# Turning q and k rows by a DMA transpose instead of TensorE, in the last stack of a one-core kernel

## The chip, the cores and the metric

The kernel runs on one NeuronCore of a Trainium2 chip, as one launch. The metric is the time on the device in microseconds. The kernel before takes 2354.93 us, the median of three runs (2354.59 to 2355.26).

## What is computed

256 tokens of width 2048, all in f32, go through two blocks. The first is a mixer (a gMLP branch and a neighbourhood attention) with a convolved feed-forward. The second has two layers, a gated delta net and a chunked band attention. The change is in that last layer. Cut to what matters:

```python
def chunk_band_attention(h, w_in, q_norm_w, k_norm_w, rel_bias, w_out):
    proj = h @ w_in                                  # 2048 -> 4 * 2048: q, k, v, z
    q = rms_norm_2(proj[..., :B_INNER].reshape(bsz, t, B_HEADS, B_HEAD_DIM), q_norm_w)
    k = rms_norm_2(proj[..., B_INNER:2 * B_INNER].reshape(...), k_norm_w)
    ...
    s = einsum('bchd,bmhd->bhcm', q_n, k_n) * scale + bias    # per chunk of 64 rows, a band of 9 chunks
    p = softmax(s)
    o = einsum('bhcm,bmhd->bchd', p, v_n) * silu(z)
    return o @ w_out
```

There are 16 heads of 128 columns, and the norm is over the 128 columns of a head. The scores contract over these columns, so q and k must lie with the columns of a head on the partitions; the projection leaves them with the tokens on the partitions.

## The kernel before

**Weights.** Every product of rows with a weight matrix is made in split precision. Weights come in halves: here 2 x 128 rows by 512 columns, 512 KB, loaded by SyncE into one of four slots of `raw` (`RAW = 4`). ScalarE copies a half to `w_hi` in fp32r (`act_half`, L494), VectorE subtracts to get `w_lo` (`dve_half`, L504), each into one of four slots (`SPLIT = 4`), and TensorE makes 12 matmuls of a half (`pe_half`, L559 to L561): three products for each of two row blocks of 128 tokens. A tile is a 512-column slice of the result over all 2048 rows of weight, 8 halves, 96 matmuls, in two PSUM banks `G[t % 2]`. SyncE loads a half when `lo_done` says that its slot is free; ScalarE splits half m when TensorE has finished half m - 4.

**Order.** Each engine has one queue, written out by hand. `run(half, n, side, group)` issues n halves and after each one takes one step of each generator given; `yield` ends a step. The generators of the engines are counted so that the steps fit together. ScalarE and VectorE are two halves ahead of TensorE in this order (`LOOK = 2`): their call c of a tile prepares its half c + 2.

**The last stack** is `stack(T_B, rows_side, band, ...)`. For each of four groups of four heads it makes four tiles: q, k, v and z, then three more groups in a loop. After the q tile has ended, `read_rows` scales it out of PSUM to `tok` (ScalarE one row block, VectorE the other), and the next tile, k, runs with `rows_side(gi, 0)` beside it; the v tile runs with `rows_side(gi, 1)`, which treats k. Below, a tile is named by the rows that are treated beside it. `band(gi)` (scores, softmax, values) starts in the z tile and is stretched over the next two tiles, so that its last steps stand beside the q rows of the next group; its first eight steps are empty.

`rows_side` before, call by call: (1) ScalarE sums the squares of `tok`; (2) VectorE makes the mean, ScalarE the root; (3) VectorE takes the reciprocal and scales `tok`, `b_normed`; (4) TensorE turns `tok` by 8 transposes into `AX[0]` and `AX[1]` (`turn_rows`, L1939), `b_turned`; (5) ScalarE copies one bank (L1157), VectorE the other (L1873), to `bqT` or `bkT`, with the norm weight of q or k as scale, `b_out0` and `b_out1`. The scores wait for these at the ninth step of `band`. ScalarE's twentieth step of `band` writes `zT_hi` (L1183), for which VectorE's `zT_lo` waits (L1917); both stand in call 4 of the tile in which the q rows are treated.

Of the kernel before, what the change touches and what calls it, by code (L numbers as in the profile page):

```python
# [13 lines left out]

F32 = mybir.dt.float32
F32R = mybir.dt.float32r
ACT = mybir.ActivationFunctionType
ALU = mybir.AluOpType
AX_X = mybir.AxisListType.X
# [2 lines left out]
P = 128  # L22
T = 256
TB = T // P
D = 2048
# [97 lines left out]
def program(nc, ins, out, parts=4):  # L123
    last_tile = {1: T_UP1, 2: T_A, 3: T_B, 4: N_TILES}[parts]
    last_half = TILE_END[last_tile - 1]
    with ExitStack() as ctx:
# [14 lines left out]
        class Region:  # L141
# [4 lines left out]

            def put(self, name, shape, dt=F32):
                t = nc.alloc_sbuf_tensor_at(name, shape, dt, offset=self.at)
                self.at += nbytes(shape)
                assert self.at <= self.end, (name, self.at, self.end)  # L150
                return t

# [145 lines left out]
        def parts_of(ap, l, h):  # L298
# [18 lines left out]
                     (ins[n][0] for n in ("w_in", "w_branch", "w_out", "w_up", "w_down", "a_w_in_2", "a_w_out_2",  # L317
                                          "b_w_in_2", "b_w_out_2"))))
        bsq = r.put("bsquares", [P, TB, 512])


        SKEW, BAND = 7 * P, 2 * P + C
        na_skew = nc.dram_tensor("na_bias_copies", (NAH, GRID, SKEW), F32, kind="Internal").ap()
        root_rows = nc.dram_tensor("root_rows", (P, TB), F32, kind="Internal").ap()
        gc_rows = nc.dram_tensor("gc_rows", (TB, H, P), F32, kind="Internal").ap()
        band_skew = nc.dram_tensor("band_bias_copies", (H, C, BAND), F32, kind="Internal").ap()

        block = ctx.enter_context(nc.Block())
# [186 lines left out]
        def pe_half(pe, pl):  # L515

            m = pl.m
            if m >= last_half:
                return
            h = HALVES[m]  # L520
            t, w = h["tile"], h["width"]
            if h["start"] and t == IN_AUX[0]:
                pe.wait_ge(S("d_v_rows"), 8)
            elif h["start"] and t == IN_AUX[1]:
                pe.wait_ge(S("b_out0"), 8)
                pe.wait_ge(S("b_out1"), 8)
            elif h["start"] and t >= 2:
                for tb in range(TB):
                    pe.wait_ge(S(f"read_out{tb}"), pl.tiles(t - 1))
            pe.wait_ge(S("lo_done"), pl.halves(m + 1))  # L530
            hi, lo = {"h": (hT_hi, hT_lo), "y": (yT_hi, yT_lo), "m": (mT_hi, mT_lo), "z": (zT_hi, zT_lo)}[h["act"]]
            _, wh, wl = slots(m)
            if is_up(t):
                def low():
                    for k in range(h["n"]):
                        for i in range(w // P):
                            nc.tensor.matmul(up_banks(t)[i][:, 0:T], wl[:, k, i * P:(i + 1) * P], hT[:, h["kt"] + k, 0, :],  # L537
                                             start=False, stop=False)

                if not h["start"]:  # L540
                    low()
                for k in range(h["n"]):
                    for i in range(w // P):
                        mm = nc.tensor.matmul(up_banks(t)[i][:, :], wh[:, k, i * P:(i + 1) * P],  # L544
                                              hT[:, h["kt"] + k, :, :].rearrange("p a t -> p (a t)"),
                                              start=h["start"] and k == 0, stop=h["stop"] and k == h["n"] - 1)
                if h["start"]:
                    for k in range(h["n"]):
                        for i in range(w // P):
                            mm = nc.tensor.matmul(up_banks(t)[i][:, 0:T], wl[:, k, i * P:(i + 1) * P], hT[:, h["kt"] + k, 0, :],  # L550
                                                  start=False, stop=False)
            order = [(k, tb) for k in range(h["n"]) for tb in range(TB)]
            if t == N_TILES - 1 and h["stop"]:
                order.sort(key=lambda at: at[1])
            for k, tb in () if is_up(t) else order:
                xh = hi[:, h["kt"] + k, tb * P:(tb + 1) * P]
                xl = lo[:, h["kt"] + k, tb * P:(tb + 1) * P]
                dst = (AX[tb] if t in IN_AUX else G[t % 2][tb])[:, 0:w]
                nc.tensor.matmul(dst, xh, wl[:, k, :], start=h["start"] and k == 0, stop=False)  # L559
                nc.tensor.matmul(dst, xh, wh[:, k, :], start=False, stop=False)  # L560
                mm = nc.tensor.matmul(dst, xl, wh[:, k, :], start=False, stop=h["stop"] and k == h["n"] - 1)  # L561
                if t == N_TILES - 1 and h["stop"] and (k, tb) == (h["n"] - 1, 0):
                    mm.then_inc(S("first_rows"), 1)
            mm.then_inc(S("half_done"), 1)
            pl.m += 1
# [111 lines left out]
        def _(act):  # L677
# [236 lines left out]
            if parts >= 2:  # L914
                act.wait_ge(S("read_out1"), T_UP1 - 3)
                act.wait_ge(S("consts_landed"), 16 * 10)
                copy_bias(band_skew, ins["b_rel_bias_2"], 2 * REL + 1, "band_copied", 0, H)
                act.dma_start(nf[:, :], ins["norm_final"].partition_broadcast(P)).then_inc(S("nf_landed"), 16)
                feed_forward(T_UP1, 0, UP1, DOWN1, 0)
                act.dma_start(alog[:, :], ins["a_a_log_2"][0].partition_broadcast(P)).then_inc(S("ab_landed"), 16)  # L920
                act.dma_start(dtb[:, :], ins["a_dt_bias_2"][0].partition_broadcast(P)).then_inc(S("ab_landed"), 16)
                act.dma_start(wab[:, :, :], W["a_in"][:, 4 * D:].rearrange("(k p) n -> p k n", p=P)).then_inc(S("wab_landed"), 16)
                feed_forward(T_UP2, UP1, UP2, DOWN2, 1)

            def sums_of_squares(src, dst, junk, event=None, after=None, blocks=range(TB)):
# [171 lines left out]
            def decays():  # L1097
# [4 lines left out]
                A(abT[:, :], AX[3][:, 0:T], ACT.Copy).then_inc(S("ab_out"), 1)  # L1102
                yield
                yield
                act.wait_ge(S("ab_landed"), 32)
                A(alog[:, :], alog[:, :], ACT.Exp)
                act.wait_ge(S("ab_sum"), 1)
                A(beta[:, :, :], gx[:, :, :], ACT.Abs)
# [34 lines left out]
            def rows_side(gi, part):  # L1143
# [7 lines left out]
                A(bss[:, :, :], bss[:, :, :], ACT.Sqrt).then_inc(S("b_root"), 1)  # L1151
                yield
                yield
                yield
                act.wait_ge(S("b_turned"), n + 1)
                for e in range(2):
                    i = A((bqT, bkT)[part][:, e, :], AX[0][:, e * T:(e + 1) * T], ACT.Copy,  # L1157
                          scale=head_gains[:, 1 + part:2 + part])
                i.then_inc(S("b_out0"), 1)
                yield  # L1160

            def band(gi):
                for _ in range(8):
                    yield
                for pr in range(2):
                    n = gi * 2 + pr
# [25 lines left out]
        def _(dve):  # L1192
# [87 lines left out]
            def mixing():  # L1280
# [10 lines left out]
                dve.wait_ge(S("gains_landed"), 16 * 4)  # L1291
                V.tensor_tensor(gains[:, 2, :], gains[:, 2, :], gains[:, 4, :], ALU.mult)
                dve.wait_ge(S("consts_landed"), 16 * 10)
                dve.wait_ge(S("ln_sd"), 1)
                V.reciprocal(lnr[:, :], lnr[:, :])
                dve.drain()
# [441 lines left out]
                e.then_inc(S("z_lo"), 1)  # L1738
                yield

            def read_rows(t, part, bufs, norm):
                if part < 3:
                    tile_done(dve, pl, t)
                    V.tensor_scalar(bufs[part][:, 1, :], G[t % 2][1][:, :], rstd[:, norm, 1:2], None,
                                    ALU.mult).then_inc(S("read_out1"), 1)

            def stack(t0, side, group, bufs, norm, first, second, out_turned):
                for part in range(3):
                    run(half, 8, second if part else none, side(0, part - 1) if part else first)
                    if part == 0:  # L1750
                        finish(first)
                    read_rows(t0 + part, part, bufs, norm)
                finish(second)
                with dve.Fori(0, 3) as i:
                    pl.enter(i, t0 + 3, 4)
# [2 lines left out]
                    for part in range(3):  # L1758
                        run(half, 8, g, side(i + 1, part - 1) if part else side(i, 2))
                        if part == 2:  # L1760
                            finish(g)
                        read_rows(t0 + 4 + part, part, bufs, norm)
                    pl.leave(3)
                g, s = group(3), side(3, 2)
                run(half, 6, g)
# [46 lines left out]
            def decays():  # L1812
# [1 line left out]
                    yield  # L1814
                ab = AX[2][:, 0:TB * 2 * H].rearrange("p (t c) -> p t c", t=TB)
                dve.wait_ge(S("ab_turned"), 1)
                dve.wait_ge(S("ab_landed"), 32)
                for tb in range(TB):
                    e = V.scalar_tensor_tensor(out=gx[:, tb, :], in0=ab[:, tb, 0:H], scalar=rstd[:, 3, tb:tb + 1], in1=dtb[:, :],
                                               op0=ALU.mult, op1=ALU.add)  # L1820
# [37 lines left out]
            def rows_side(gi, part):  # L1858
                n = gi * 2 + part
                if part == 2:  # L1860
# [8 lines left out]
                scaled(tok, tok, bss[:, :, :]).then_inc(S("b_normed"), 1)  # L1869
                yield  # L1870
                yield
                dve.wait_ge(S("b_turned"), n + 1)
                V.tensor_scalar((bqT, bkT)[part][:, 2:4, :], AX[1][:, :].rearrange("p (a t) -> p a t", a=2),  # L1873
                                head_gains[:, 1 + part:2 + part], None, ALU.mult).then_inc(S("b_out1"), 1)
                yield

            def band(gi):
# [49 lines left out]
        def _(pe):  # L1927
# [372 lines left out]

            def decays():

                pe.wait_ge(S("wab_landed"), 16)
                for kt in range(0, KD, 4):
                    for h_part in (hT_hi, hT_lo):
                        for j in range(4):
# [39 lines left out]
                finish(turn_x(2, 3, T_A - 1))  # L2346

            def rows_side(gi, part):
                if part == 2:
                    return  # L2350
                n = gi * 2 + part
                yield
                yield
                yield
                pe.wait_ge(S("b_normed"), n + 1)
                if not isinstance(gi, int) or gi or part:
                    pe.wait_ge(S("b_out0"), n)
                    pe.wait_ge(S("b_out1"), n)
                turn_rows(tok, (0, 1), "b_turned")
                yield  # L2360
                yield

            def band(gi):
                for _ in range(8):
                    yield
                for pr in range(2):
                    n = gi * 2 + pr
                    if pr == 0:
                        pe.wait_ge(S("b_out0"), gi * 2 + 2)
                        pe.wait_ge(S("b_out1"), gi * 2 + 2)  # L2370
                        pe.wait_ge(S("read_out0"), gi * 4 + (T_B + 3))
                        pe.wait_ge(S("read_out1"), gi * 4 + (T_B + 3))
                        pe.wait_ge(S("z_lo"), gi + 4)
# [79 lines left out]
```

## Time and profile before

| | before |
|---|---|
| median of 3 runs | 2354.93 us |
| profiled execution: span from first to last instruction | 2353.4 us |
| own time of the profiled execution | not recorded apart; all runs are within 2354.59 to 2355.26 us |
| TensorE busy | 2343.1 us |
| VectorE busy | 1516.3 us |
| ScalarE busy | 1223.8 us |
| weight and other loads, main DMA queue | 57.6% of 16 engines |

Times in the profile are microseconds from the start of the span. PE is TensorE's matmuls, PEld its weight loads, DVE is VectorE, ACT is ScalarE, ACTq and SPq are the instructions of a queue that issue DMAs. In a timeline a row gives start, duration, engine, line, operation, output and inputs, count, and in brackets the idle time before it with what ended it. Matmuls are pipelined: their durations overlap, and their starts give the pace.

### The profile page before, as it was taken

The page shows a single profiled execution, that of the slowest core. Times are in us where ns is not written, and L with a number is a line of the kernel's source. Part 1 is how long each engine was busy: PE and PEld are TensorE (multiplying, and loading weights), DVE is VectorE, ACT ScalarE, POOL GpSimd, SP SyncE. Part 2 cuts the span into 40 slices and gives each one's busy share as a digit, 9 for nine tenths or more (in the row PEclk, how much of TensorE's full clock was granted, in tenths as well). Part 3 has the DMA queues.
Part 4 walks back from the last instruction along what each step waited for, and adds up shares of the span by engine and source line. Part 5 has one row for each costly group of instructions (what it writes and reads, how often), then busy time and mean ns, then how long its engine had stood idle before and what let it go on. Part 6 is the DMA issues. An engine that isn't in the chain of part 4 may idle for free.

```text
span 2353.4 us, 35087 instructions
## 1 busy us (share of the span) xinstructions
PE 2343.1 (100%) x12183; PEld 1963.4 (83%) x12183; DVE 1516.3 (64%) x2146; ACT 1223.8 (52%) x1931; POOL 68.7 (3%) x92
## 2 busy tenths in 40 slices
PE   9999999999999999999999999999999999999999
PEld 7887788888888888888888878888887888888887
DVE  5657655556577775477776668787876755555554
ACT  5445544444465554355554475756465455555543
POOL 0011200000200000000000000000000000000000
PEclk9999999999999999999999999999999999999999
DMA  8665555565656656566655655555554575656555
GB/s 272 219 207 178 171 190 190 180 200 185 222 179 196 193 183 199 182 196 188 194 184 189 192 154 169 153 169 151 161 149 148 180 223 163 193 155 187 169 169 171
DMA packets 289497, 432.66 MB, mean 184 GB/s; under 512 B 32976, under 2 KB 129136, under 8 KB 289264
## 3 DMA queue, kind: packets, MB, share of 16 engines
q1 hardware_dynamic: 282976, 422.69, 57.6%
q10 hardware_dynamic: 6416, 8.56, 1.1%
q8 instruction: 66, 1.08, 0.2%
q14 instruction: 39, 0.32, 0.0%
HBM read 429.07 MB, written 7.10 MB: 185 GB/s over the span
## 4 chain that ended last, share of the span: by engine, by line
PE 95%; DVE 2%; ACT 1%; DVEq 1%; issue 0%; DMA 0%; ACTq 0%
PE gemm L559 22%; PE gemm L561 22%; PE gemm L560 22%; PE gemm L544 7%; PE aux L544 7%; PE gemm L537 3%; PE aux L537 3%; PE aux L1939 2%; DVE w_lo L504 1%; PE aux L561 1%; PE aux L560 1%; PE aux L559 1%; ACT w_hi L494 1%; PE aux L2180 0%; PE aux L2399 0%; PE aux L2380 0%
## 5 line engine op out<-in xcount | busy, mean ns | idle before, releaser
L504 DVE TENSOR_TENSOR w_lo<-raw,w_hi 128x1024 fp32r<-128x1024 f32 (+1 forms) x800 | 958.1, 1206 | 572.3 <-ACT w_hi L494 567.4
L494 ACT ACTIVATE w_hi<-raw 128x1024 fp32r<-128x1024 f32 (+1 forms) x800 | 815.6, 1042 | 506.0 <-PE gemm L561 402.7
L559 PE MATMUL gemm<-w_lo,hT 128*128 128x512 f32 x1600 | 637.0, 398 | 0.7 <-DVE hT L1224 0.6
L561 PE MATMUL gemm<-w_hi,hT 128*128 128x512 f32 x1600 | 624.0, 390 | 0.0
L560 PE MATMUL gemm<-w_hi,hT 128*128 128x512 f32 x1600 | 623.3, 390 | 0.0
L559 PEld LDWEIGHTS gemm<-w_lo,hT 128*128 128x128 f32 x1600 | 300.6, 188 | 64.8 <-issue 4.1
L561 PEld LDWEIGHTS gemm<-w_hi,hT 128*128 128x128 f32 x1600 | 300.3, 188 | 63.8
L560 PEld LDWEIGHTS gemm<-w_hi,hT 128*128 128x128 f32 x1600 | 300.8, 188 | 58.8 <-issue 0.2
L544 PE MATMUL gemm<-hT,w_hi 128*128 128x512 f32 x704 | 218.5, 393 | 0.1
L544 PE MATMUL aux<-hT,w_hi 128*128 128x512 f32 x672 | 208.0, 390 | 0.0
L559 PE MATMUL gemm<-w_lo,yT_hi 128*128 128x512 f32 x472 | 184.3, 390 | 0.5 <-DVE yT_lo L1467 0.5
L561 PE MATMUL gemm<-w_hi,yT_lo 128*128 128x512 f32 x472 | 183.7, 389 | 0.0
L560 PE MATMUL gemm<-w_hi,yT_hi 128*128 128x512 f32 x472 | 183.6, 389 | 0.0
L544 PEld LDWEIGHTS aux<-hT,w_hi 128*128 128x128 f32 x672 | 126.2, 188 | 28.5
L544 PEld LDWEIGHTS gemm<-hT,w_hi 128*128 128x128 f32 x704 | 122.3, 190 | 17.0 <-issue 0.5
L537 PE MATMUL gemm<-hT,w_lo 128*128 128x256 f32 x616 | 122.1, 282 | 0.0
L537 PE MATMUL aux<-hT,w_lo 128*128 128x256 f32 x588 | 118.5, 283 | 0.0
L537 PEld LDWEIGHTS gemm<-hT,w_lo 128*128 128x128 f32 x616 | 103.9, 190 | 10.2
L559 PEld LDWEIGHTS gemm<-w_lo,yT_hi 128*128 128x128 f32 x472 | 88.6, 188 | 19.8 <-DVE yT_lo L1467 0.9
L561 PEld LDWEIGHTS gemm<-w_hi,yT_lo 128*128 128x128 f32 x472 | 88.6, 188 | 18.6
L560 PEld LDWEIGHTS gemm<-w_hi,yT_hi 128*128 128x128 f32 x472 | 88.6, 188 | 18.1
L537 PEld LDWEIGHTS aux<-hT,w_lo 128*128 128x128 f32 x588 | 91.3, 191 | 0.0
(341 smaller groups left out, 2283.4 us busy)
## 6 DMA issues: line engine op xcount, KB each, us to landing
raw<-in_w_up SPq DMA_DIRECT2D x336, 256.0 KB, 2.9
raw<-in_w_in SPq DMA_DIRECT2D x144, 512.0 KB, 4.4
raw<-in_a_w_in SPq DMA_DIRECT2D x128, 512.0 KB, 3.6
raw<-in_b_w_in SPq DMA_DIRECT2D x128, 512.0 KB, 4.2
raw<-in_w_down SPq DMA_DIRECT2D x76, 512.0 KB, 4.6
raw<-in_w_branch SPq DMA_DIRECT2D x32, 512.0 KB, 4.5
raw<-in_w_out SPq DMA_DIRECT2D x32, 512.0 KB, 4.7
raw<-in_a_w_out SPq DMA_DIRECT2D x32, 512.0 KB, 3.7
```

Source lines behind the costliest of these rows:

```text
L494: nc.scalar.activation(hi, src, ACT.Copy).then_inc(S("hi_done"), 1)
L504: nc.vector.tensor_tensor(lo, src, hi.bitcast(F32), ALU.subtract).then_inc(S("lo_done"), 1)
L537: nc.tensor.matmul(up_banks(t)[i][:, 0:T], wl[:, k, i * P:(i + 1) * P], hT[:, h["kt"] + k, 0, :], start=False, stop=False)
L544: mm = nc.tensor.matmul(up_banks(t)[i][:, :], wh[:, k, i * P:(i + 1) * P], hT[:, h["kt"] + k, :, :].rearrange("p a t -> p (a t)"), start=h ...
L559: nc.tensor.matmul(dst, xh, wl[:, k, :], start=h["start"] and k == 0, stop=False)
L560: nc.tensor.matmul(dst, xh, wh[:, k, :], start=False, stop=False)
L561: mm = nc.tensor.matmul(dst, xl, wh[:, k, :], start=False, stop=h["stop"] and k == h["n"] - 1)
L1939: m = turn(AX[b][:, e * T + tb * P:e * T + (tb + 1) * P], src[:, tb, c:c + P], ident[:, :])
```

## The change

`tok`, once scaled, is split by ScalarE into two planes of 16-bit halves of each f32 word. They are written to DRAM as `row_planes_kept` (2, 256, 2, 512), so that the low and the high half of a token's row are two rows of 512. A DMA transpose then reads those 512 rows of 512 two-byte elements back, with the columns on the partitions; since the rows alternate low and high, the halves lie side by side in SBUF and are f32 words again, in `bqT` or `bkT`. TensorE's transposes of `tok` and the four PSUM reads with their norm weights are gone. Neither q nor k is scaled by its own norm weight any more: the product of both is put on `bkT` by one instruction a group, in the third step of ScalarE's `band`, and the scores wait for that (`b_gained`). VectorE waits for `b_planes` before it overwrites `tok`. Apart from that, the last aux tile no longer waits for anything of its own, and the semaphore `wab_landed` is merged into `ab_landed`, whose readers wait for three loads.

```diff
+        planes = r.put("row_planes", [P, TB, 2, 512], U16)
+        turn_mark = r.put("turn_mark", [P, 1])
...
+        row_planes = nc.dram_tensor("row_planes_kept", (2, T, 2, 512), U16, kind="Internal").ap()
...
             if h["start"] and t == IN_AUX[0]:
                 pe.wait_ge(S("d_v_rows"), 8)
-            elif h["start"] and t == IN_AUX[1]:
-                pe.wait_ge(S("b_out0"), 8)
-                pe.wait_ge(S("b_out1"), 8)
-            elif h["start"] and t >= 2:
+            elif h["start"] and t >= 2 and t not in IN_AUX:
...
-                act.dma_start(wab[:, :, :], W["a_in"][:, 4 * D:].rearrange("(k p) n -> p k n", p=P)).then_inc(S("wab_landed"), 16)
+                act.dma_start(wab[:, :, :], W["a_in"][:, 4 * D:].rearrange("(k p) n -> p k n", p=P)).then_inc(S("ab_landed"), 16)
...
@@ ScalarE, rows_side
                 A(bss[:, :, :], bss[:, :, :], ACT.Sqrt).then_inc(S("b_root"), 1)
                 yield
                 yield
-                yield
-                act.wait_ge(S("b_turned"), n + 1)
-                for e in range(2):
-                    i = A((bqT, bkT)[part][:, e, :], AX[0][:, e * T:(e + 1) * T], ACT.Copy,
-                          scale=head_gains[:, 1 + part:2 + part])
-                i.then_inc(S("b_out0"), 1)
+                act.wait_ge(S("b_normed"), n + 1)
+                words = tok[:, :, :].bitcast(U16).rearrange("p t (c w) -> p t w c", w=2)
+                for w in range(2):
+                    e = A(planes[:, :, w, :], words[:, :, w, :], ACT.Copy)
+                e.then_inc(S("b_planes"), 1)
+                act.wait_ge(S("b_planes"), n + 1)
+                act.dma_start(row_planes[part].rearrange("(t p) w c -> p t (w c)", p=P),
+                              planes[:, :, :, :].rearrange("p t w c -> p t (w c)")).then_inc(S("b_written"), 16)
+                yield
+                yield
+                act.wait_ge(S("b_written"), n * 16 + 16)
+                A(turn_mark[:, :], ones[:, 0:1], ACT.Copy)
+                act.dma_start_transpose((bqT, bkT)[part][:, :, :].bitcast(U16),
+                                        row_planes[part].rearrange("t w c -> (t w) c")).then_inc(S("b_turned"), 16)
                 yield
@@ ScalarE, band
-                for _ in range(8):
+                yield
+                yield
+                act.wait_ge(S("b_turned"), gi * 32 + 32)
+                A(bkT[:, :, :], bkT[:, :, :], ACT.Copy, scale=head_gains[:, 3:4]).then_inc(S("b_gained"), 1)
+                for _ in range(6):
                     yield
@@ VectorE
+                V.tensor_tensor(head_gains[:, 3:4], head_gains[:, 1:2], head_gains[:, 2:3], ALU.mult)
...
+                    if not isinstance(planes_read, int) or planes_read:
+                        dve.wait_ge(S("b_planes"), planes_read)
...
                 scaled(tok, tok, bss[:, :, :]).then_inc(S("b_normed"), 1)
                 yield
                 yield
-                dve.wait_ge(S("b_turned"), n + 1)
-                V.tensor_scalar((bqT, bkT)[part][:, 2:4, :], AX[1][:, :].rearrange("p (a t) -> p a t", a=2),
-                                head_gains[:, 1 + part:2 + part], None, ALU.mult).then_inc(S("b_out1"), 1)
                 yield
@@ TensorE, rows_side
-                pe.wait_ge(S("b_normed"), n + 1)
-                if not isinstance(gi, int) or gi or part:
-                    pe.wait_ge(S("b_out0"), n)
-                    pe.wait_ge(S("b_out1"), n)
-                turn_rows(tok, (0, 1), "b_turned")
+                return none
@@ TensorE, band
-                        pe.wait_ge(S("b_out0"), gi * 2 + 2)
-                        pe.wait_ge(S("b_out1"), gi * 2 + 2)
+                        pe.wait_ge(S("b_gained"), gi + 1)
```

## Rows read from the trace of the kernel before

**Rows 1.** The page: span, busy times by engine, shares of the chain.
```profile
span 2353.4 us, 35087 instructions
PE 2343.1 (100%) x12183; PEld 1963.4 (83%) x12183; DVE 1516.3 (64%) x2146; ACT 1223.8 (52%) x1931; POOL 68.7 (3%) x92
...
PE 95%; DVE 2%; ACT 1%; DVEq 1%; issue 0%; DMA 0%; ACTq 0%
```
**Rows 2.** Windows of the last stack: busy by engine, granted clock, DMA share, GB/s.
```profile
2013.00:2036.00 23.00, 23.00 (x107) 19.14 (x106) 12.46 (x13) 12.41 (x29) 0.00 (x0) 1.00 0.62 193
2082.00:2105.00 23.00, 23.00 (x122) 19.55 (x121) 16.11 (x30) 15.23 (x39) 0.00 (x0) 1.00 0.50 147
```
**Rows 3.** Timeline of TensorE in the tile beside k rows.
```profile
2017.76 0.39 PE L559 MATMUL gemm<-w_lo,hT 128*128 128x512 f32 x1
...
2028.41 0.39 PE L561 MATMUL gemm<-w_hi,hT 128*128 128x512 f32 x1
2028.64 1.03 PE L1939 MATMUL aux<-ident,tok 128*128 128x128 f32 x8
2029.43 0.48 PE L559 MATMUL gemm<-w_lo,hT 128*128 128x512 f32 x1
2029.75 0.39 PE L560 MATMUL gemm<-w_hi,hT 128*128 128x512 f32 x1
...
2040.42 0.39 PE L559 MATMUL gemm<-w_lo,hT 128*128 128x512 f32 x1
```
**Rows 4.** Chain in order of time (start, us, what): first and last of 8 such rows.
```profile
1909.55 0.87 PE aux L1939 x8
...
2221.94 0.87 PE aux L1939 x8
```
**Rows 5.** Timelines of ScalarE, then VectorE, in the same tile.
```profile
2024.68 2.96 ACT L494 ACTIVATE w_hi<-raw 128x1024 fp32r<-128x1024 f32 x3
2029.71 0.84 ACT L1157 ACTIVATE bkT<-aux,head_gains 128x256 f32<-128x256 f32 x2 [2.07 <-PE aux L1939]
2030.44 1.06 ACT L494 ACTIVATE w_hi<-raw 128x1024 fp32r<-128x1024 f32 x1
...
2041.21 3.20 ACT L494 ACTIVATE w_hi<-raw 128x1024 fp32r<-128x1024 f32 x3
...
2027.19 1.23 DVE L1502 TENSOR_TENSOR tok<-tok,brow_squares 128x1024 f32<-128x1024 f32 x1
...
2030.60 0.74 DVE L1873 TENSOR_SCALAR bkT<-aux,head_gains 128x512 f32<-128x512 f32 x1
```
**Rows 6.** DMA issues with KB each and microseconds to landing; the main queue; gc_all's instructions.
```profile
q1 hardware_dynamic: 282976, 422.69, 57.6%
...
raw<-in_b_w_in SPq DMA_DIRECT2D x128, 512.0 KB, 4.2
...
bias<-na_bias_copies SPq DMA_DIRECT2D x32, 96.0 KB, 3.9
...
gc_all<-gc_rows ACTq DMA_DIRECT2D x3, 512.0 KB, 5.6
out_rows<-x_rows SPq DMA_DIRECT2D x6, 256.0 KB, 5.1
...
out_rows<-x_rows SPq DMA_DIRECT2D x4, 128.0 KB, 1.9
...
L992 ACTq DMA_DIRECT2D gc_all<-gc_rows x3: 389/399/422, 1425.5 to 1642.5; - x3
...
DMA to landing us min/median/max: 5.4/5.6/5.9
```
**Rows 7.** Timelines of ScalarE, VectorE, TensorE beside q rows with a band.
```profile
2100.09 1.09 ACT L1183 ACTIVATE zT_hi<-aux 128x512 f32 x2 [0.31 <-PE aux L1939]
...
2100.27 1.23 DVE L1502 TENSOR_TENSOR tok<-tok,brow_squares 128x1024 f32<-128x1024 f32 x1
...
2102.55 1.28 DVE L1917 TENSOR_TENSOR zT_lo<-aux,zT_hi 128x512 f32 x2
2103.75 1.21 DVE L504 TENSOR_TENSOR w_lo<-raw,w_hi 128x1024 fp32r<-128x1024 f32 x1
...
2114.32 0.39 PE L559 MATMUL gemm<-w_lo,hT 128*128 128x512 f32 x1
```

More of the change, by code:

```diff
@@ L16 @@
 F32R = mybir.dt.float32r
+U16 = mybir.dt.uint16
 ACT = mybir.ActivationFunctionType
@@ L148, in put @@
                 t = nc.alloc_sbuf_tensor_at(name, shape, dt, offset=self.at)
-                self.at += nbytes(shape)
+                self.at += nbytes(shape) // (2 if dt == U16 else 1)
                 assert self.at <= self.end, (name, self.at, self.end)
@@ L1104, in decays @@
                 yield
-                act.wait_ge(S("ab_landed"), 32)
+                act.wait_ge(S("ab_landed"), 16 * 3)
                 A(alog[:, :], alog[:, :], ACT.Exp)
@@ L1739, in delta, with read_rows @@
                 yield
-            def read_rows(t, part, bufs, norm):
+            def read_rows(t, part, bufs, norm, planes_read=0):
                 if part < 3:
                     tile_done(dve, pl, t)
+                    if not isinstance(planes_read, int) or planes_read:
+                        dve.wait_ge(S("b_planes"), planes_read)
                     V.tensor_scalar(bufs[part][:, 1, :], G[t % 2][1][:, :], rstd[:, norm, 1:2], None,
@@ L1751, in stack @@
                         finish(first)
-                    read_rows(t0 + part, part, bufs, norm)
+                    read_rows(t0 + part, part, bufs, norm, part if norm == 4 and part < 2 else 0)
                 finish(second)
@@ L1761, in stack @@
                             finish(g)
-                        read_rows(t0 + 4 + part, part, bufs, norm)
+                        read_rows(t0 + 4 + part, part, bufs, norm, i * 2 + (2 + part) if norm == 4 and part < 2 else 0)
                     pl.leave(3)
@@ L1816, in decays @@
                 dve.wait_ge(S("ab_turned"), 1)
-                dve.wait_ge(S("ab_landed"), 32)
+                dve.wait_ge(S("ab_landed"), 16 * 3)
                 for tb in range(TB):
@@ L2301, in decays @@
             def decays():
-                pe.wait_ge(S("wab_landed"), 16)
+                pe.wait_ge(S("ab_landed"), 16 * 3)
                 for kt in range(0, KD, 4):
@@ L2348, in rows_side @@
             def rows_side(gi, part):
-                if part == 2:
-                    return
-                n = gi * 2 + part
-                yield
-                yield
-                yield
-                pe.wait_ge(S("b_normed"), n + 1)
-                if not isinstance(gi, int) or gi or part:
-                    pe.wait_ge(S("b_out0"), n)
-                    pe.wait_ge(S("b_out1"), n)
-                turn_rows(tok, (0, 1), "b_turned")
-                yield
-                yield
+                return none
             def band(gi):
```

## Prediction

> **What bounds the kernel.** I read the page's busy line and its chain of waits first. TensorE is busy for 2343.1 of 2353.4 us, and the chain that ends last runs through it for 95% [rows 1]. The granted clock is 1.00 in the stretches I looked at, the higher of the two levels, 2.4 GHz [rows 2]. So a microsecond of TensorE work taken away is a microsecond gained, as long as the two engines that prepare weights keep up: ScalarE writes `w_hi` (1.06 us a half), VectorE then `w_lo` (1.2 us), and TensorE takes a half every 2.72 us: from 2017.76 to 2028.64 it does four of them, 48 matmuls 0.2267 us apart [rows 3]. What decides here is how far ahead those two are where the change puts work and waits into their queues. That I read in the timelines, tile by tile.
>
> **What goes.** In the last stack q and k of each head group are turned by 8 transposes, 8 blocks in all [rows 4]. The chain counts 0.87 us for a block. In the timeline the last matmul ahead of a block starts at 2028.41 and the first behind it at 2029.43, 1.02 us where 0.227 is usual; the matmul after that comes 0.32 later in place of 0.227 [rows 3]. That is 0.79 + 0.09 = 0.88 us. The tile as a whole: from 2017.76 to 2040.42 are 22.66 us; eight halves at 2.72 are 21.76; so 0.90 [rows 3]. 8 x 0.90 = 7.2 us, all on the path. ScalarE loses a pair of PSUM reads (0.84 us) and VectorE one (0.74 us) per block [rows 5]; neither engine sets the end, so that counts only as slack. The merged `ab_landed` count is waited for long after its three loads; nothing. `b_out0` and `b_out1` were long raised where the aux tile starts, nothing either. The product of the two norm weights is one column, made in the first stage: nothing.
>
> **What comes, per q or k (8 times).** On ScalarE: two plane copies of 128x1024. No 2-byte copy with a stride is in the trace; the nearest row is the split of the same count of elements, 1.06 us each and 2.96 for three in a row [rows 5], so about 2.0 to 2.1 us for two. Below, they could be half of that if two-byte output were faster; above, I allow 3.1 for reads at a stride. Then a DMA issue, later a wait for its landing, a marker of 0.2 us and the issue of the transpose. Once a group a gain over all of `bkT`, 128x1024, 1.1 us.
>
> **Does that stay hidden? The k tile,** 2017.76 to 2040.42. VectorE ends the scaling of the rows at 2028.42 [rows 5]; this doesn't move, since nothing ahead of it changes. ScalarE, idle then, copies planes until 2030.6, issues at 2030.7 (0.40 us, the issue of `gc_all` [rows 6]), and is free at 2031.1. Before, it was free for the next split at 2030.44. The tile's seventh half is split 2031.1 to 2032.15 and its `w_lo` is ready at 2033.4. TensorE, 0.90 us earlier now, wants it at 2034.1 (2040.42 - 0.90 - 2 x 2.72). It holds by 0.7 us. The eighth half follows at once. Then ScalarE waits for the write. Call L its landing time, x the time for which the transpose's issue keeps ScalarE's queue. The marker and the waits take 0.25, the split 1.06, `w_lo` 1.25: the next tile's first half is ready at 2030.7 + L + 0.25 + x + 2.3 = 2033.25 + L + x, and TensorE wants it at 2039.52. **So L + x may be 6.3 us; beyond that every microsecond is one of TensorE.** Five of the eight cases look so (four k, and the first q).
>
> **The q tile with a band beside it,** ended at 2114.32 (three cases). Here the scaling ends at 2101.50 and ScalarE's `zT_hi`, which stood at 2100.09, now queues behind planes and issue [rows 7]. Planes until 2103.6, issue until 2104.2, `zT_hi` until 2105.3, the seventh half's `w_hi` until 2106.3. VectorE's `zT_lo` waits for it: 2105.35 to 2106.6, then `w_lo` until 2107.8; before, that was 2103.75 to 2104.96. Wanted at 2114.32 - 0.90 - 5.44 = 2108.0. It holds by 0.2 us: a planes pair of 3.1 us would cost 0.8 us here, three times, 2.4 in all. The next tile's first half is ready at 2103.8 + L + 0.25 + x + 2.3, wanted at 2113.4: L + x may be 7.0.
>
> **L.** Only five rows are near. A DMA of the same 512 KB from ScalarE's queue, beside the weights, lands in 5.4 to 5.9 us; weights of 512 KB in 4.2; a store of 256 KB in 5.1, and one of 128 KB at the quiet end in 1.9 [rows 6]. Lower bound 4.2, upper 6.5 (a store of twice the 256 KB), and I take 5.4: same size, same queue, same neighbours, its shortest time, since the write's 256 rows of 2 KB are half the reads' count.
>
> **x.** The trace has no DMA transpose. From below: 0.40 us like the other issue. From above: if the queue works a transpose off block by block, 16 blocks of 128x128 at 0.39 are 6.2 us. I take 0.5, since it is one instruction and even 512 KB cost one issue 0.4 us; but this is the weakest number here. With L = 5.4 and x = 0.5 the sum is 5.9, under both limits: no stall.
>
> **The transpose's own landing.** It is wanted when ScalarE, three splits into the z tile, waits for `b_turned`. It gets there at about 2044 (three splits, 3.2 us, that begin at 2041.21 now and 0.9 earlier then [rows 5]); TensorE needs the sixth half of that tile at 2039.5 + 13.6 = 2053.1, so split and `w_lo` may start at 2050.8 and the gain at 2049.7. Issued at about 2036.5, it has **13 us of cover**; q has a tile more. From below it lands like `gc_all`, 5.6 us; from above, 16 blocks one after another at the 1.9 us of the smallest store, 30 us. I take the lower side: it moves the same 512 KB, and DMA runs of 256 bytes are nothing special here, since the `bias` loads, which consist of them, land in 3.9 us [rows 6]. Its load on the engines: all DMA of 57.6% of 16 engines over 282976 packets is 77 ns a packet; 2048 pieces of 256 bytes at no more than that are 9.8 us of all 16 engines, at most. The k stretch leaves 38% of 23 us, 8.7 us, idle [rows 2], and a weight load may land some 4 us later than now (four slots, 10.9 us of pace, 2.3 of splitting) before ScalarE notices at all. So I cost contention at nothing; without that cover it would be some 2 us a time.
>
> One rule of the Trainium skill speaks against this reading: "VectorE: DVE Perf Modes", in the section on the three transpose paths, gives a 128x128 DMA transpose 1309 ns against 390 on TensorE. Sixteen in a row would be, as an estimate from that page, 21 us, 8 beyond the cover, four times: a sum of +25 us in place of -7. "DMA: Bandwidth & Descriptors", in its section on latency, has 261 GB/s for a DMA transpose, 2 us for this one by estimate, and the sum stays. No row here decides between the two.
>
> **Sum.** -7.2 on the path, +0 for planes, issue and waits where all holds. The profiled span is 2353.4 against a median of 2354.93; 1.5 us lie outside the span, and stay. 2354.9 - 7.2 = 2347.7; I add 0.3 for a thin margin missed now and then: **2348.0**.
>
> **Rivals.** A difference under 0.2% (4.7 us) is about what a measurement of this kernel can't tell from none.
> - *A. All hidden*, 2348, from 2347.3 to 2350.0 (stalls up to 2.3 us in all). For it: the sums above. 46%.
> - *B. The write's landing eats the gain.* L + x between 6.8 and 8.0: at 7.3 five stalls of 1.0 and three of 0.3 give 5.9 us, 2353.6. For it: margins of 0.2 to 0.7 us, and reads of this size at 5.9. 19%, within 0.2%.
> - *C. The transpose's issue holds ScalarE's queue; slower.* The place is the last split ahead of the tile's end, the price 8 us for each microsecond of x beyond 1.6, once the limits are passed. It decides from about x = 2.7; at 2.8, with L = 5.4, five times 1.9 and three times 1.2 are 13 us, 2361. At x = 6.2: 5 x 5.3 + 3 x 4.6 = 40 us, 2388. For it: one instruction for 16 blocks; nothing like it in the trace. Against: an issue of 512 KB costs 0.4 us whatever its count of rows. 24%.
> - *D. The transpose lands late.* Nothing below 13 us, then four microseconds each: at 21 us it gives 4 x 8 = 32, so 2380; at 30 us 68, so 2416. The reading of VectorE's page above is this case. With it goes the starving of weights. 11%.
>
> **Range and chances.** Below 2347 nothing leads, since the gain is bounded by the eight blocks. C reaches 2388, and D beyond it. I leave out most of D and what lies below: 2347.0 to 2388. The likeliest case alone has 2347.3 to 2350.0. Faster by over 0.2%: A, 0.46. Within: B, 0.19. Slower: C and D, 0.35.
>
> **What would show it.** In the profile after: no transposes of `tok` in the last stack, and a k tile of 21.8 us in place of 22.66. Plane copies of about 1.05 us. A `row_planes` write that lands in 5 to 6 us. ScalarE's queue held 0.4 to 0.5 us by the transpose, and TensorE idle nowhere before the first half of a tile. If instead `w_lo` of that half is what TensorE waits for, the interval of the transpose's issue tells C from B. If it waits in the z tile, behind the gain, it is D; if `w_hi` waits for `raw`, it is contention. The prediction is wrong if x is over 2 us or a transpose takes over 13.

## The result, and the profile after

The changed kernel takes 2364.35 us, the median of four runs (2360.66 to 2368.93), against 2354.81: a ratio of 1.0040, 95% interval 1.0028 to 1.0052. It is slower by 9.5 us, where 6.9 us of gain were forecast: the time lies inside the stated range, but the kernel became slower where it was to become faster. Its runs spread over 8 us, those of before over 0.7. The profiled execution took 2362.43 us, its span is 2360.7: 7.3 us above the span of before [rows 1].

The page, against [rows 1]: the chain ran through TensorE for 95%, and now through it for 89%, with ScalarE's queue and a DMA in it.

```profile
span 2360.7 us, 34978 instructions
PE 2340.6 (99%) x12119; PEld 1958.5 (83%) x12119; DVE 1510.3 (64%) x2139; ACT 1237.6 (52%) x1943; POOL 65.1 (3%) x92
...
PE 89%; DVE 3%; ACT 3%; DMA 2%; ACTq 1%; issue 1%; DVEq 1%
```

The tile table, in which the new instructions are named with minimum, median and maximum in ns, and the landing below each in microseconds. The plane copies, the write, then the two transposes:

```profile
L1158 ACT ACTIVATE row_planes<-tok x16: 1040/1050/1059, 1908.8 to 2228.8; 128x1024 uint16<-128x1024 uint16 x16
L1161 ACTq DMA_DIRECT2D row_planes_kept<-row_planes x8: 383/388/416, 1910.8 to 2229.9; - x8
...
DMA to landing us min/median/max: 4.4/4.5/6.3
```
```profile
...
L1167 ACTq DMA_TRANSPOSE bqT<-row_planes_kept x4: 3516/3657/6004, 1916.2 to 2211.1; - x4
...
DMA to landing us min/median/max: 7.1/7.2/8.1
```
```profile
...
L1167 ACTq DMA_TRANSPOSE bkT<-row_planes_kept x4: 2587/3508/3886, 1942.1 to 2234.3; - x4
...
DMA to landing us min/median/max: 4.7/6.0/6.5
```

The plane copies take 1.05 us, as taken; the write's issue 0.39, its landing 4.4 to 6.3, median 4.5. What is new is the transpose: its issue holds ScalarE's queue for 2.6 to 6.0 us. Where that goes is seen in the waits of the last stack (who waited for whom, total, times, longest):

```profile
DVE w_lo L508 <- ACT w_hi L498: 163.5, 83, 8.6
...
ACT w_hi L498 <- issue: 19.3, 5, 5.9
ACT turn_mark L1166 <- DMA row_planes_kept<-row_planes: 15.9, 8, 3.8
...
PE gemm L560 <- DVE w_lo L508: 10.3, 7, 4.6
...
ACT w_hi L498 <- DMA raw<-in_b_w_in: 6.0, 5, 1.9
```

TensorE, which waited for nothing in the last stack before, waits 7 times for `w_lo`, 10.3 us in all. The longest is the first; timelines of ScalarE, VectorE and TensorE:

```profile
1910.84 0.40 ACTq L1161 DMA_DIRECT2D row_planes_kept<-row_planes  x1
1911.34 2.01 ACT L498 ACTIVATE w_hi<-raw 128x1024 fp32r<-128x1024 f32 x2 [0.53 <-ACT row_planes L1158]
1916.15 0.20 ACT L1166 ACTIVATE turn_mark<-ones 128x1 f32<-128x1 f32 x1 [2.80 <-DMA row_planes_kept<-row_planes]
1916.15 6.00 ACTq L1167 DMA_TRANSPOSE bqT<-row_planes_kept  x1
1922.26 2.00 ACT L498 ACTIVATE w_hi<-raw 128x1024 fp32r<-128x1024 f32 x2 [5.91 <-issue]
```
```profile
1912.43 2.36 DVE L508 TENSOR_TENSOR w_lo<-raw,w_hi 128x1024 fp32r<-128x1024 f32 x2 [2.53 <-ACT w_hi L498]
1923.35 2.36 DVE L508 TENSOR_TENSOR w_lo<-raw,w_hi 128x1024 fp32r<-128x1024 f32 x2 [8.56 <-ACT w_hi L498]
```
```profile
1919.71 0.39 PE L562 MATMUL gemm<-w_hi,hT 128*128 128x512 f32 x1
1924.72 0.76 PE L560 MATMUL gemm<-w_lo,hT 128*128 128x512 f32 x1 [4.62 <-DVE w_lo L508]
1925.28 0.63 PE L561 MATMUL gemm<-w_hi,hT 128*128 128x512 f32 x1
1925.71 0.63 PE L562 MATMUL gemm<-w_hi,hT 128*128 128x512 f32 x1
```

The write is issued at 1910.84, has landed at 1916.15 (L = 5.3), and the transpose then keeps the queue until 1922.15 (x = 6.0). ScalarE's next split stands behind it, `w_lo` behind the split, and TensorE, done with the tile at 1920, starts at 1924.72. Its matmuls are then 0.43 us apart (1925.28 to 1925.71) in place of 0.227, and the windows say why (columns: PE, PEld, DVE, ACT, POOL busy with counts, granted clock, DMA share, GB/s):

```profile
1918.00:1924.70 6.70, 2.10 (x10) 1.42 (x9) 1.35 (x2) 2.44 (x3) 0.00 (x0) 0.86 1.01 171
1924.70:1929.00 4.30, 4.28 (x10) 3.43 (x11) 2.80 (x3) 3.68 (x19) 0.00 (x0) 0.50 0.72 227
1929.00:1930.00 1.00, 1.00 (x4) 0.76 (x4) 0.17 (x1) 0.80 (x1) 0.00 (x0) 0.69 0.91 223
1930.00:1935.00 5.00, 5.00 (x23) 4.13 (x23) 3.70 (x6) 2.22 (x3) 0.00 (x0) 1.00 1.04 264
```

After 4.6 idle microseconds the granted clock is 0.50, the lower level of 1.2 GHz, for at least 4.3 us. As an estimate, half of the 4.3 us is lost, 2.15 us, and the slices around it some 0.3 more. So the difference of 7.3 us is: -7.2 for the eight blocks, which are gone as forecast, +10.3 idle, +2.5 of lower clock, and 1.7 left. As an estimate that is the price of seven restarts at about 0.25 us: around the idle stretch of 0.62 us at 2022, two matmuls start 1.01 us apart where 0.227 is usual, 0.78 lost, and the next start comes 0.11 late, 0.27 us beyond the idle time in all.

The transpose also fills the DMA engines. In the window from 1918.00 they are busy for a share of 1.01 while they move 171 GB/s; in the tile of [rows 2] a share of 0.62 moved 193 GB/s.

### The profile page after: what moved, and what is told of

The parts are those of the page before. It is cut to its first block, busy times and chain, and to the rows that moved or that the text cites. A ratio compares the mean times of both kernels' runs of the same rounds, so it can differ in the third digit from the quotient of the medians.

```text
span 2360.7 us, 34978 instructions
## 1 busy us (share of the span) xinstructions
PE 2340.6 (99%) x12119; PEld 1958.5 (83%) x12119; DVE 1510.3 (64%) x2139; ACT 1237.6 (52%) x1943; POOL 65.1 (3%) x92
## 3 DMA queue, kind: packets, MB, share of 16 engines
q10 hardware_dynamic: 25232, 16.95, 2.7%
## 4 chain that ended last, share of the span: by engine, by line
PE 89%; DVE 3%; ACT 3%; DMA 2%; ACTq 1%; issue 1%; DVEq 1%
PE gemm L560 20%; PE gemm L562 20%; PE gemm L561 20%; PE gemm L545 7%; PE aux L545 7%; PE gemm L538 3%; PE aux L538 3%; DVE w_lo L508 2%; PE aux L1952 1%; DMA row_planes_kept<-row_planes 1%; ACT w_hi L498 1%; ACTq L1167 1%; PE aux L561 1%; PE aux L562 1%; PE aux L560 1%
## 5 line engine op out<-in xcount | busy, mean ns | idle before, releaser
L560 PE MATMUL gemm<-w_lo,hT 128*128 128x512 f32 x1600 | 638.0, 399 | 10.4 <-DVE w_lo L508 10.3
L545 PEld LDWEIGHTS aux<-hT,w_hi 128*128 128x128 f32 x672 | 126.2, 188 | 28.5
L538 PEld LDWEIGHTS gemm<-hT,w_lo 128*128 128x128 f32 x616 | 103.9, 190 | 10.3
```

## The experiments

Each ratio below is to the kernel before as it ran on the same chip, with its 95% interval; its median was 2354.8 to 2355.1 us in every such group of runs.

### e1: an ordinary DMA in the transpose's place

```diff
-                words = tok[:, :, :].bitcast(U16).rearrange("p t (c w) -> p t w c", w=2)
+                words = tok[:, :, :].bitcast(U16).rearrange("p t (w c) -> p t w c", w=2)
...
-                act.dma_start_transpose((bqT, bkT)[part][:, :, :].bitcast(U16),
-                                        row_planes[part].rearrange("t w c -> (t w) c")).then_inc(S("b_turned"), 16)
+                act.dma_start((bqT, bkT)[part][:, :, :].bitcast(U16)...,
+                              row_planes[part].rearrange("(t p) w c -> p t (w c)", p=P)).then_inc(S("b_turned"), 16)
```

> Edit: the DMA transpose is replaced by an ordinary DMA of the same 512 KB from the same DRAM tensor to the same tile, in the same place of ScalarE's queue; the plane copies read their halves in order, so that words stay whole. Left out: q and k are not turned. Planes, write, wait for the write, marker and gain stay. Theory H (in the changed kernel the transpose's issue holds ScalarE's queue for 2.6 to 6.0 us): the issue takes 0.4 us, TensorE idles nowhere in the last stack, time about 2348. Rival W (the wait for the write and the plane copies cost the time, whatever is issued behind them): still about 2360 to 2364. Rival D (the transpose's traffic slows the weights): also 2348, so H and D are told apart by e2 and e4.

Measured: 2349.67 us, ratio 0.9976 (0.9966 to 0.9985). The tile table, q's DMA:

```profile
L1167 ACTq DMA_DIRECT2D bqT<-row_planes_kept x4: 371/372/377, 1918.2 to 2201.0; - x4
DMA to landing us min/median/max: 4.1/4.7/6.1
```

The issue takes 0.37 us, and TensorE idles for 0.62 and 0.35 us, twice in all, where the write landed late (median 5.6 here). The forecast of no idle time missed by these two. Theory H holds otherwise: planes, write and the wait for it are hidden but for thin margins, and the transpose made the difference to 2364. The plane copies read contiguous halves here and take 1.05 us all the same (1.04 to 1.06), so the edit to them changes nothing. This run can't tell whether the transpose costs by its issue or by its traffic.

An ordinary DMA of 512 KB here is 272 packets, the transpose 2080: the page's count for ScalarE's queue is 6416 before, 10768 in e1 (eight writes and eight reads) and 25232 in the changed kernel. The number of pieces alone doesn't make a long issue. The kernel before loads `w_ab` from ScalarE's queue, 2048 rows of 128 bytes in one ordinary DMA, and its issue takes 0.46 us:

```profile
L922 ACTq DMA_DIRECT2D w_ab<-in_a_w_in x1: 460/460/460, 982.8 to 982.8; - x1
DMA to landing us min/median/max: 4.7/4.7/4.7
```

### e2: the transpose two splits later

```diff
+                yield
+                yield
                 yield
                 yield
                 act.wait_ge(S("b_written"), n * 16 + 16)
```

> Edit: ScalarE's wait for the write, the marker and the transpose's issue stand in call 8 of the tile instead of call 6, two splits later, just ahead of the read of the finished tile, for which ScalarE waits 4.4 us anyway. Nothing left out. H: the issue still takes 2.6 to 6.0 us, but lies in that wait; the first halves of the next tile are split before it; no idle time but perhaps some at the 6.0 us one; 2348 to 2350. D: the same traffic at nearly the same time, so stalls stay and the time is about 2360. Rival late landing: k's transpose is issued some 2 us later with 13 us of cover, lands in 5 to 8, so nothing.

Measured: 2358.26 us, ratio 1.0016 (1.0005 to 1.0026). That is near what rival D said, and not H; the waits show that D has most of it, not all. The waits of the last stack, and the transposes of q:

```profile
ACT w_hi L498 <- DMA raw<-in_b_w_in: 28.5, 15, 5.4
...
PE gemm L560 <- DVE w_lo L508: 9.0, 9, 2.2
```
```profile
L1169 ACTq DMA_TRANSPOSE bqT<-row_planes_kept x4: 2982/3722/7137, 1916.5 to 2211.4; - x4
DMA to landing us min/median/max: 11.2/14.6/20.2
```

ScalarE's splits wait 28.5 us for weights (6.0 in the changed kernel), and q's transposes land in 11 to 20 us (7.1 to 8.1 there). The nine pieces, from the timelines: 1.7, 2.2 and 1.7 us behind splits that had waited 3.2 to 3.9 us for weights, and three of 0.4 to 0.6 at the next split behind each of these, 7.2 us in all. The first two, 1.15 and 0.45, are of the issue: it lasted 7.14 us, longer than the wait of 4.4 us that was to hide it. The last, 0.23, follows a gain that had waited for k's transpose. Those landed in 7.4 to 13.8 us and ScalarE waited for them 7.3 us in three pieces, so the forecast of 5 to 8 us for their landing missed too.

In this version SyncE's loads and the transpose are in flight together. In the changed kernel they mostly were not: ScalarE, held by the issue, made no split, so no slot came free and SyncE issued no load. SyncE's timeline in the changed kernel, around its first transpose:

```profile
1913.68 1.50 SPq L361 DMA_DIRECT2D raw<-in_b_w_in  x2
1915.23 0.58 SPq L443 DMA_DIRECT2D bbias<-band_bias_copies  x1
1924.60 1.50 SPq L361 DMA_DIRECT2D raw<-in_b_w_in  x2
```

No load is issued between 1915.8 and 1924.60, while the transpose is issued from 1916.15 to 1922.15; nor is one from 1941.6 to 1948.6, around the issue of the first k at 1942.15. Two things were open: whether the contention is the transpose's or that of any 512 KB, and whether the issue on its own is harmless on another queue.

### e3: half the transpose

```diff
-                act.dma_start_transpose((bqT, bkT)[part][:, :, :].bitcast(U16),
-                                        row_planes[part].rearrange("t w c -> (t w) c")).then_inc(S("b_turned"), 16)
+                act.dma_start_transpose((bqT, bkT)[part][:, 0:2, :].bitcast(U16),
+                                        row_planes[part][:, :, 0:256].rearrange("t w c -> (t w) c")).then_inc(S("b_turned"), 16)
```

> Edit: only the first 256 of the 512 columns are turned (256 KB), in the same place as in the changed kernel; heads 2 and 3 of each group use the q and k of heads 0 and 1 in the scores. Left out: half the turning, half the gain. H with an issue in proportion to the blocks turned: 1.3 to 3 us, median 1.8; with the write's 4.5 us the sum is 6.3, at the limit: stalls of 0 to 1 us, time 2348 to 2351. H with an issue of fixed length: as the changed kernel, about 2360 to 2364.

Measured: 2351.43 us, ratio 0.9987 (0.9978 to 0.9996). The issue:

```profile
L1167 ACTq DMA_TRANSPOSE bqT<-row_planes_kept x4: 1256/1262/1339, 1917.6 to 2201.9; - x4
```

The issue takes 1.26 us, with a spread of 0.08 where the whole spread over 3.4. The size matters, and half the columns cost less than half of the whole's median; in proportion it would have been 1.8. TensorE idles twice, 1.36 and 0.49 us, with a write that landed in 5.0 us at the median and not in 4.5, and the time is just above the forecast of 2348 to 2351.

### e4: the transpose issued by SyncE

```diff
@@ SyncE, tile(): after the load of the fifth half of the tile that follows the one beside which the rows are treated
+                    if turned is not None and k == 8:
+                        sp.dma_start_transpose((bqT, bkT)[turned][:, :, :].bitcast(U16),
+                                               row_planes[turned].rearrange("t w c -> (t w) c")).then_inc(S("b_turned"), 16)
@@ ScalarE, rows_side
                 act.wait_ge(S("b_written"), n * 16 + 16)
                 A(turn_mark[:, :], ones[:, 0:1], ACT.Copy)
-                act.dma_start_transpose(...)
```

The load ahead of it waits for the `w_lo` of the tile's first half, which ScalarE splits behind its wait for the write; so the order write, transpose is kept.

> Edit: the transpose is issued by SyncE, behind the load of the next tile's fifth half, instead of by ScalarE; ScalarE keeps its wait for the write and the marker in call 6. Nothing left out. H: SyncE's queue is held for 3 to 6 us in place of ScalarE's; the weight loads behind it start that much later, which four slots cover (8 us before ScalarE notices, 5 more before TensorE does); no idle time, 2348. W: stays at 2360. D: stays at 2360, or w_hi waits for raw for several us a time.

Measured: 2348.95 us, ratio 0.9974 (0.9964 to 0.9983). TensorE idles once, 0.79 us. The issue is as long as before, on the other queue:

```profile
L363 SPq DMA_TRANSPOSE bqT<-row_planes_kept x4: 3195/3412/4245, 1921.6 to 2203.8; - x4
DMA to landing us min/median/max: 5.4/5.9/7.2
```

H holds: the same transpose, with an issue of 3.2 to 4.2 us, costs next to nothing where the queue it holds has slack. And q's lands in 5.4 to 7.2 us, k's in 5.3 to 5.4. That fits with the loads standing behind it in the same queue; no run separates this from the later place of the transpose.

### e5: e2 with an ordinary DMA

Edit: the DMA of e1, in call 8 as in e2.

> Edit: as e1 (an ordinary DMA of the same 512 KB in place of the transpose) and as e2 (wait, marker and issue in call 8). Left out: q and k are not turned. Tells what spoiled e2, where the transposes landed in 7 to 20 us, w_hi waited 28.5 us for raw, and the time was 2358. Theory T (a transpose and the weight loads behind it slow each other, an ordinary DMA doesn't): w_hi waits for raw under 6 us in all, as in e1; 2348 to 2350. Rival P (any 512 KB at this place, where loads run at full pace, are too many): w_hi waits for raw as in e2, 2355 to 2358.

Measured: 2347.96 us, ratio 0.9970 (0.9959 to 0.9981); TensorE idles nowhere in the last stack. The wait for weights is

```profile
ACT w_hi L498 <- DMA raw<-in_b_w_in: 5.4, 7, 1.4
```

against 28.5 us in e2. Same bytes, same place, same loads beside it: the contention comes with the transpose. The windows from 1924 to 1936, in e2 and then in e5, show how the DMA engines fared:

```profile
1924.00:1936.00 12.00, 10.32 (x43) 7.54 (x41) 5.10 (x6) 6.64 (x22) 0.00 (x0) 1.00 1.13 161
```
```profile
1924.00:1936.00 12.00, 12.00 (x55) 9.94 (x54) 6.75 (x8) 8.03 (x13) 0.00 (x0) 1.00 1.00 272
```

With the transpose they are no less busy (a share of 1.13 against 1.00; it is the summed time of the packets and can pass 1) and move 161 GB/s in place of 272. The longest landing of a weight load is 18.2 us in e2 and 11.6 in e5. One rival is open: the ordinary DMA moves its 512 KB in 272 packets and the transpose in 2080, so an ordinary DMA of as many small pieces might crowd the weights as well. No run has one at this place.

### e6: two transposes of 256 columns, a split between them

```diff
+                act.dma_start_transpose((bqT, bkT)[part][:, 0:2, :]..., row_planes[part][:, :, 0:256]...)
+                yield
+                act.dma_start_transpose((bqT, bkT)[part][:, 2:4, :]..., row_planes[part][:, :, 256:512]...)
```

> Edit: the transpose is two of 256 columns each, the first in call 6, the second in call 7, one split of weights between them. Nothing left out. e3 had 1.25 us for the issue of such a half, with hardly any spread, where the whole took 2.6 to 6.0. Theory Q (an issue has a fixed rate, some 2.5 us for the whole; the rest is the queue filling up and waiting for the data to move): each half 1.25 us, the split between them keeps TensorE fed, 2349 to 2352. Rival (the second half finds the first in the way): the first 1.25, the second 2 to 4 us, TensorE idle some 5 us in all, 2355 or more.

Measured: 2353.82 us, ratio 0.9996 (0.9987 to 1.0005). The issues of q's, first and second half:

```profile
L1167 ACTq DMA_TRANSPOSE bqT<-row_planes_kept x4: 1257/1294/1340, 1916.6 to 2204.4; - x4
L1170 ACTq DMA_TRANSPOSE bqT<-row_planes_kept x4: 1675/2073/3238, 1918.1 to 2205.9; - x4
```

The first takes 1.25 to 1.34 us always; the second up to 3.2 for q, and 1.24 to 1.73 for k. TensorE idles 4.5 us in seven pieces. The time falls between both forecasts: an issue of 256 columns has a price of 1.25 us, and a second one behind it is sometimes held up.

### e7 and e9: four small transposes back to back

Edits: e7 has four pieces of 512 rows by 128 columns, e9 four of 128 rows by 512 columns, all in call 6.

> Edit: the transpose is four of 128 columns each, back to back in call 6. Nothing left out. Theory Q: the first two take about 0.65 us each, those behind them more, since the queue is full; the sum is as the whole's, 3.6 us, and the time as the changed kernel's, 2360 to 2364. Rival (the whole is slow because it is one large instruction): all four at 0.65 us, sum 2.6, time 2352 to 2355.

> Edit: the transpose is four of 128 source rows by all 512 columns each, back to back in call 6; e7 had four of 512 rows by 128 columns, 1.29 us each, while a half of 512 rows by 256 columns took 1.25 as well. Nothing left out. Theory R (an issue is paid by its rows, for up to 256 columns at a time): a piece has a quarter of the rows and two lots of columns, 0.3 x 2 = 0.6 to 0.7 us, four are 2.6 us with the queue's waiting on top, 2355 to 2362. Rival F (an issue has a fixed price of about 1.2 us, plus little for its size): four at 1.2 or more, 5 us in all, 2375 to 2380 as e7.

Measured: e7 2379.58 us, ratio 1.0105 (1.0089 to 1.0120); e9 2378.20 us, ratio 1.0101 (1.0084 to 1.0118). Issues of q's pieces, first and last of four, in e7 and then in e9:

```profile
L1167 ACTq DMA_TRANSPOSE bqT<-row_planes_kept x4: 1155/1157/1227, 1917.0 to 2221.1; - x4
...
L1173 ACTq DMA_TRANSPOSE bqT<-row_planes_kept x4: 1293/1294/1295, 1920.9 to 2224.9; - x4
```
```profile
L1167 ACTq DMA_TRANSPOSE bqT<-row_planes_kept x4: 1222/1226/1304, 1917.8 to 2222.2; - x4
...
L1173 ACTq DMA_TRANSPOSE bqT<-row_planes_kept x4: 1298/1300/1301, 1921.8 to 2226.1; - x4
```

Theory Q (0.65 us a piece) and theory R are both refuted; rival F is what is seen. 128 KB cost 1.14 to 1.31 us in either shape, and 256 KB (e3, e6) cost 1.25 too. So an issue has a floor of about 1.2 us that its size didn't lower here, and four of them, 5.0 to 5.2 us, hold the queue longer than the one whole did at its median. TensorE idles in all eight tiles, 20.2 us in e7 and 19.2 in e9. Both also show the second price, the granted clock, though not behind every stall. In e7 it falls behind the idle stretches of 4.35, 3.63 and 2.56 us of the first three q, and stays at 1.00 behind the other five, of which the longest are 2.56 and 2.35 us; in e9 it falls behind all four of q, of 2.5 to 5.5 us. Windows of e7, the first stall and what follows:

```profile
1920.00:1924.70 4.70, 0.39 (x2) 0.00 (x0) 1.33 (x2) 2.42 (x3) 0.00 (x0) 0.98 0.76 113
1924.70:1930.00 5.30, 5.26 (x17) 4.21 (x18) 2.96 (x4) 4.51 (x19) 0.00 (x0) 0.70 0.79 246
```

### e8: e4, with ScalarE's wait one call later

```diff
@@ ScalarE: one more yield ahead of act.wait_ge(S("b_written"), ...)
@@ SyncE
-                    if turned is not None and k == 8:
+                    if turned is not None and k == 10:
```

> Edit: as e4 (the transpose issued by SyncE), with ScalarE's wait for the write one call later (7) and the transpose behind the load of the sixth half instead of the fifth. Nothing left out. Theory H: what idle time e4 has left (0.8 us, where the write landed late) goes; 2347.7 to 2349. Rival: the later landing of k's transpose is waited for in the z tile; 2350 or more.

Measured: 2347.82 us, ratio 0.9970 (0.9958 to 0.9981); 2347.60 to 2348.68 over seven runs. TensorE idles nowhere in the last stack. ScalarE waits for k's transpose in the z tile, and that costs nothing:

```profile
ACT bkT L1178 <- DMA bkT<-row_planes_kept: 8.9, 4, 4.2
```

The issue holds SyncE's queue for 4.9 to 5.5 us for q and 4.0 to 5.1 for k, longer than in e4, and TensorE waits for nothing behind it. Of the kernels here that compute the whole this has the lowest median: 7.3 us below before, and 16.5 below the changed one. It differs from e4 by 1.1 us, with intervals that overlap.

## Why the prediction was wrong

**The step that failed is x**, the time for which the transpose's issue keeps ScalarE's queue. I took 0.5 us, from the issue of an ordinary DMA of as many bytes, and called it the weakest number. It measured 2.6 to 6.0, median about 3.6. ScalarE's next split stood behind it, `w_lo` behind the split, and TensorE waited 10.3 us for `w_lo`; with the issue off ScalarE's queue (e4, e8) that wait is 0.8 us or none. Rival C named this mechanism, its place and its size, and had 0.24. Its upper bound of 6.2 us lies near the longest measured by luck: it was counted at 0.39 a block, and eight blocks cost 1.25 us (e3), as much as four (e7, e9), where 0.39 each gives 3.1; in e2 one issue passed it, with 7.1.

**The limits held.** L + x could be 6.3 us (four k and the first q) or 7.0 (three q beside a band). From the timeline rows of the eight transposes, with a stall counted as the idle time plus 0.25 for the restart: the first q, 5.3 + 6.0 = 11.3, so 5.0 forecast, 4.9 measured; the other q, 8.1, 8.0 and 8.1, so 1.1, 1.0 and 1.1 forecast, 0.9, 0.8 and 0.8 measured; k, 8.9, 7.8 and 8.2, so 2.6, 1.5 and 1.9 forecast, 2.1, 1.0 and 1.5 measured. The first k had 9.0 and no stall where 2.7 were forecast. It comes behind the largest one, in a tile in which TensorE lost 2.5 us to the lower clock, so ScalarE had about that much more time; this fits, and wasn't tested apart. With the measured medians (L = 4.5, x = 3.6) my formula gives 5 x 1.8 + 3 x 1.1 = 12.3 us of stalls, 2360.0. The median is 4.4 above that, and the formula has no term for the granted clock: 2.5 us in the profiled execution. Where the slower runs lost more isn't known, since only one was profiled; their mean granted clock goes from 0.999 in the fastest to 0.997 in the slowest.

**The gain** of 7.2 us was right: e8, in which nothing stalls, is 7.3 below before, and e5 7.2.

**Planes and write** were right in kind and size: copies of 1.05 us (taken: 1.06), a write of 4.4 to 6.3 us (taken 5.4, from 4.2 to 6.5). That the margin is thin shows in e1 (L of 5.6 at the median, two stalls under a microsecond); with the wait one call later (e8) no stall is left. Rival B was therefore there, but worth under 2 us (e1 against e5, 2349.67 and 2347.96), not 6.

**The transpose's landing** (rival D): it lands in 4.7 to 8.1 us in the changed kernel, inside the 13 of cover. By the Trainium skill, "VectorE: DVE Perf Modes", section on the three transpose paths, the estimate was 21 us, and by the Trainium skill, "DMA: Bandwidth & Descriptors", section on latency, it was 2 us. The 4.7 to 8.1 us measured lie between, and neither was met. I costed contention with the weights at nothing by the count of packets; e2 shows that this was wrong as an argument. In the changed kernel little of it is seen (6.0 us of waits for weights), because the same issue that stalls TensorE also keeps the loads back. Once ScalarE is no longer held at that point, the contention appears (28.5 us of waits for weights); with the transpose on SyncE's queue the waits for weights are 7.1 us (e4) and 3.5 (e8), and the loads stand behind the transpose there.

**What stays open:** what the queue does for 1.2 us at the least, and why a whole transpose takes from 2.6 to 6.0, and to 7.1 in e2. The shortest, 2.59 us, is about two pieces of 256 columns at 1.25. That the longest falls where SyncE also loads `bbias` suggests waiting for DMA traffic; this was not isolated. Whether the weights are crowded by the turning or by the 2080 small packets is open as well.

## What to carry to other kernels

A DMA is not free for the queue that issues it, and an instruction of another kind has an issue price of its own: count it as work on that engine, and where no row shows it, give the bound that decides more weight than the nearest row. Put a long issue on the queue whose lateness costs least; here that is the loading queue, four slots ahead, where the loads also stand behind the transpose. And a stall of TensorE of some microseconds can be paid twice, once idle and once at the lower clock behind it, as behind 4.6 us in the changed kernel.

## What the runs showed of the hardware

- The issue of a DMA transpose holds its queue for 1.14 to 1.34 us at 128 KB and at 256 KB (apart from a second one that was held up, to 3.2), and for 2.6 to 7.1 us at 512 KB; an ordinary DMA of 512 KB held ScalarE's queue in the last stack for 0.37 to 0.43, and one of 2048 rows of 128 bytes for 0.46.
- A transpose of 512 KB is 2080 packets, an ordinary DMA of the same bytes 272.
- A transpose in flight together with weight loads landed in 11 to 20 us (e2, q), and one issued from the queue of the loads in 5.4 to 7.8 (e4 and e8, q). An ordinary DMA of the same bytes among the same loads landed in 4.6 to 9.9 (e5, q). With the transpose among them the DMA engines moved 161 GB/s at a share of 1.13, with the ordinary DMA 272 at 1.00.
- After an idle stretch of 4.6 us the granted clock was 0.50 for the next 4.3 us; behind the other six of the changed kernel, 0.6 to 1.9 us, it stayed at 1.00. In e7 it fell behind one stretch of 2.56 us and not behind another.
- A copy of two-byte elements that reads every second one takes ScalarE 1.05 us for 128x1024, about as the contiguous f32 split does (1.06) and a contiguous two-byte copy (1.05, e1).
